# Layer 1's projection back: places freed for its first weights, most of the mixed output split in the attention's last steps, residual read in two parts

## The chip, the cores and the metric

The kernel runs on one core of a Trainium2 chip. The metric is the device time of one execution in microseconds (us); lower is better. Five engines work beside each other, each through its own queue of instructions in order, and meet only at semaphores: PE (matrix products), ACT (activations), DVE (elementwise), POOL (elementwise, slower) and SP, which here only issues DMAs.

## The reference

Two blocks run one after the other on x of 1024 tokens by 1024 features, all in float32. The first block has two layers; the second of them, layer 1, is the one that is touched:

```python
def odd_mixer(h, w_in, sink, w_out, slopes):
    proj = h @ w_in
    qc, kc, vc, gc = jnp.split(proj, [C_Q, C_Q + C_KV, C_Q + 2 * C_KV], axis=-1)
    oc = windowed_sink_attention(qc, kc, vc, sink, slopes)   # 16 heads, 4 key heads, window of 3 blocks of 128
    return (oc * jax.nn.silu(gc)) @ w_out                     # 1024 x 1024
...
x = x + gate * y            # the residual, for which x is needed again
return rms_norm(x, final_norm)
```

The score of a head is q k / 8 plus a bias, minus slope times distance; a sink enters the maximum and the sum. The second block (a recurrence, a gated linear attention, a feed-forward part) follows and is not touched.

## The kernel before, in words

**Split products.** Every product is made of three: a float32 operand is split into a rounded "high" part (fp32r) and the remainder, the "low" part, and PE adds high x high, low x high and high x low. A projection works through output tiles of 128 features. For each, SP loads weights of 128 x 1024 into WR (`sp_weights`), ACT rounds them into WH (`act_high`), POOL makes the remainder WL (`pool_low`), and PE runs 8 steps k with 6 matmuls each of 128x512 (`pe_tile`). WR, WH and WL have two slots each; tile t uses slot t % 2, and its sums lie in two of PSUM's eight banks. `sp_weights(t)` waits until WL of tile t-2 is made.

**The attention of layer 1** (`*_attention_c`) has NG = 32 groups g (4 key heads by 8 blocks of 128 queries) of two units u each (NU = 64). Each engine walks one loop over u, in which the steps of several units are interleaved: in step u PE does the scores of u, turns the probabilities of u-1, spreads the inverse sums of (u-3)/2 and multiplies with the values of group (u-4)/2; DVE adds the bias (`dve_c_bias`), makes the low part of the probabilities (`dve_c_low`), multiplies the gate with the inverse sum (`dve_c_gate`, into C_G) and adds the two halves of the output (`dve_c_add`, into C_O2); ACT does the exponentials (`act_c_raise`, into C_PR), the high part (`act_c_high`) and moves half of the output (`act_c_move`, into C_OT); POOL widens the inverse sums and writes the product of C_O2 and C_G to MIX (`pool_c_mix`, signal c_mixed). After step 63 the loops run on for a few steps until group 31 is done. POOL also makes the bias tables BF and the low parts of keys, queries and values.

MIX, 128 partitions by 8 x 1024, is the mixed output. Its eighths f = 2i and 2i+1 belong to key head i: they are complete when group 8i+7 is.

**The projection back** (`*_odd_out`, tiles ODD_OUT[0] to [7], called tile 0 to 7 here). Tile 0's weights lie in slot 0. It starts when all of MIX is made: `act_odd_out` and `dve_odd_out` first wait for c_mixed(31). ACT then rounds tile 0's weights and the eighths of MIX into HH; DVE clears two buffers, then makes the remainders HL (signal m_low); PE starts step k of tile 0 when m_low(k) is there. SP loads tile 0's weights during the attention, waits for c_mixed(31), issues the reload of the residual X from DRAM ("spill", 4 MB in one DMA), and then the weights of tiles 1 to 7. X lies where the queries of the attention were, so it can't come earlier. DVE adds the residual to each finished tile (`dve_residual`, L398), ACT squares the result, DVE sums the squares for the norm.

**The order of work** is written out by hand: there is no planner. What one engine's instruction needs of another is a wait on a semaphore. Places in SBUF are given in KB per partition by `place(name, kb, shape)`: slot 0 of WH is 127.5 to 131.5, slot 0 of WL 135.5 to 139.5; before the change they are overlaid by BF1 (127.5) and C_PR (133.5).

Of the kernel before, what the change touches and what calls it, by code (L numbers as in the profile page):

```python
# [7 lines left out]
F32 = mybir.dt.float32  # L8
F32R = mybir.dt.float32r
# [122 lines left out]
def build(nc, d, where, known):  # L132
# [111 lines left out]
    def pe_tile(t, high, low, made=None, beside=None):  # L244
        s, w = t % 2, tiles[t]
        pe.wait_ge(*w_low.at(t))
        if t >= 2:
            pe.wait_ge(*evicted(t - 2))
        for k in range(w.kt):
            if made:  # L250
                pe.wait_ge(*made(k))
            for n, (wt, x) in enumerate(((WH, high), (WH, low), (WL, high))):
                for h in range(2):
                    last = pe.matmul(ps[0:w.m, 2 * s + h, :], wt[:, s, k, 0:w.m], x[:, k, halves(h)],  # L254
                                     start=(k == 0 and n == 0), stop=(k == w.kt - 1 and n == 2))
            if k == w.kt - 1:
                last.then_inc(*w_used.up(t))
            if beside:
                beside(k)
# [1134 lines left out]

    NG = C_KV * TT
    NU = 2 * NG
    C_KH, C_KL = place("C_KH", 59, [P, C_KV, SEQ], F32R), place("C_KL", 143.5, [P, C_KV, SEQ], F32R)
    C_QH, C_QL = place("C_QH", 159.5, [P, 4, SEQ], F32R), place("C_QL", 3, [P, DT, SEQ], F32R)
    C_VS = place("C_VS", 175.5, [P, 2, TT, P], F32R)
    C_PTH, C_PTL = place("C_PTH", 183.5, [P, 2, 3, 4, P], F32R), place("C_PTL", 195.5, [P, 2, 3, 4, P], F32R)  # L1400
    C_SB, C_PR = place("C_SB", 51, [P, 4, WIN + 1]), place("C_PR", 133.5, [P, 4, WIN + 1])
    C_OT, C_O2 = place("C_OT", 139.53125, [P, HALF]), [place("C_O20", 141.53125, [P, 2 * P]), place("C_O21", 117.75, [P, 2 * P])]
    AWAY, C_RID, C_G = place("AWAY", 75, [P, WIN]), place("C_RID", 76.5, [P, 2 * P]), place("C_G", 77.5, [P, 2, 2 * P])
    BF = [place("BF0", 111.5, [P, 4, WIN]), place("BF1", 127.5, [P, 4, WIN])]
    C_RS, C_RI, C_NM = (place(n, 117.5 + 0.03125 * i, [P, 2, 4]) for i, n in enumerate(("C_RS", "C_RI", "C_NM")))
    c_tables = signal("c_tables")
    c_scored, c_turned, c_spread, c_summed = signal("c_scored"), signal("c_turned"), signal("c_spread"), signal("c_summed")
# [47 lines left out]
    def pe_c_turn(u):  # L1455
        p = u % 2
        lo, hi, _ = window(u // 2 % TT)
        nk = hi - lo
        pe.wait_ge(*c_raised.at(u, 1))
        if u >= 2:  # L1460
            pe.wait_ge(*c_low.at(u - 2))
        for j in range(2):
            for k in range(nk):
                last = pe.transpose(ps[:, 2 + 2 * p + j, rows(k)], C_PR[:, 2 * p + j, rows(3 - nk + k)], IDENT[:, :])
        last.then_inc(*c_turned.up(u))

    def pe_c_spread(g):
# [33 lines left out]
    def dve_c_bias(u, j):  # L1501

        g, hd = u // 2, 2 * (u % 2) + j
        i, n = g // TT, g % TT
        lo, hi, b0 = window(n)
        w = (hi - lo) * P
        dve.wait_ge(*c_scored.at(u, j))
        if u >= 2:
            dve.wait_ge(*c_raised.at(u - 2, j))
        if n == 0:  # L1510
            dve.wait_ge(*c_bias.at(i, hd))
        dve.tensor_tensor_reduce(C_SB[:, hd, WIN - w:WIN], ps[:, j, 0:w], BF[i % 2][:, hd, b0:b0 + w], -1.0,
                                 NSINK[:, 4 * i + hd:4 * i + hd + 1], ALU.add, ALU.min,
                                 C_NM[:, g % 2, hd:hd + 1]).then_inc(*c_biased.up(u, j))

# [37 lines left out]
    def dve_attention_c():  # L1553
        dve.wait_ge(*c_tables.at(2))
        dve.tensor_scalar(NSINK[:, :], SINK[:, :], -1.0, None, ALU.mult).then_inc(*c_sinks.up())
        for r in range(2):
            dve.wait_ge(*c_key_high.at(0, r))
            dve.tensor_tensor(C_KL[rows(r, HD), 0, :], KC[0:HD, 0, :], C_KH[0:HD, 0, :].bitcast(F32),
                              ALU.subtract).then_inc(*c_key_low0.up(0, r))
        for t in range(2):  # L1560
            dve.wait_ge(*c_query_high.at(t))
            dve.tensor_tensor(C_QL[:, t, :], QC[:, t, :], C_QH[:, t, :].bitcast(F32), ALU.subtract).then_inc(
                *c_query_low0.up(t))
        dve.wait_ge(*c_sinks.at())
        for u in range(NU + 6):
            if u % 2 == 0 and 2 <= u <= NU:
                dve_c_inverse((u - 2) // 2)
            if u < NU:
                dve_c_bias(u, 0)
                dve_c_bias(u, 1)  # L1570
            if 2 <= u < NU + 2:
                dve_c_low(u - 2)
            if u % 2 == 0 and 4 <= u < NU + 4:
                dve_c_gate((u - 4) // 2)
            if u % 2 == 1 and 5 <= u < NU + 5:
                dve_c_add((u - 5) // 2)

    def act_c_keys(i):
        base = (i % 2) * HD
# [14 lines left out]
    def act_c_raise(u, j):  # L1594
        g, hd = u // 2, 2 * (u % 2) + j
        lo, hi, _ = window(g % TT)
        c0 = WIN - (hi - lo) * P
        act.wait_ge(*c_biased.at(u, j))
        if u >= 2:
            act.wait_ge(*c_turned.at(u - 2))  # L1600
        act.activation(C_PR[:, hd, c0:WIN + 1], C_SB[:, hd, c0:WIN + 1], ACT.Exp, bias=C_NM[:, g % 2, hd:hd + 1], scale=-1.0,  # L1601
                       accum_out=C_RS[:, g % 2, hd:hd + 1]).then_inc(*c_raised.up(u, j))

    def act_c_high(u):
# [6 lines left out]
    def act_c_move(g):  # L1611
        act.wait_ge(*c_summed.at(g))
        act.activation(C_OT[0:HD, :], ps[HD:P, 6, :], ACT.Copy).then_inc(*c_moved.up(g))

    def act_attention_c():
        act.wait_ge(*vc_copied.at(1))
        act_c_keys(0)
        for t in range(2):
            act_c_query(t)
        for u in range(NU + 5):  # L1620
            if u % 16 == 0 and u < NU:
                act_c_sinks(u // 16)
                act.wait_ge(*c_sink.at(u // 16))
            if u < NU:
                act_c_raise(u, 0)
                act_c_raise(u, 1)
            if 1 <= u <= NU:
                act_c_high(u - 1)
            if u % 2 == 0 and 4 <= u < NU + 4:
                act_c_move((u - 4) // 2)  # L1630
            i = u // 16 + 1
            if i < C_KV:
                if u % 16 == 5:
                    act_c_keys(i)
                elif u % 16 in (7, 9):
                    act_c_query(2 * i + (u % 16 - 7) // 2)
# [11 lines left out]
    def pool_c_bias(i, hd):  # L1648
        if i >= 2:
            pool.wait_ge(*c_biased.at(16 * (i - 1) - 1, 1))  # L1650
        c_pool_in_turn()
        pool.tensor_scalar(BF[i % 2][:, hd, :], AWAY[:, :], SLOPE[:, 4 * i + hd:4 * i + hd + 1], None, ALU.mult).then_inc(
            *c_bias.up(i, hd))

    def pool_c_keys(i):
# [29 lines left out]
    def pool_attention_c():  # L1685
# [6 lines left out]
        for u in range(NU + 6):  # L1692
# [5 lines left out]
            if i < C_KV:  # L1698
                if u % 16 in (1, 2, 3, 4):
                    pool_c_bias(i, u % 16 - 1)  # L1700
                elif u % 16 == 6:
                    pool_c_keys(i)
                elif u % 16 in (8, 10):
                    pool_c_query(2 * i + (u % 16 - 8) // 2)
                elif u % 16 == 12:
                    pool_c_values(i)

    SQG = place("SQG", 47, [P, 3, SEQ])  # L1710
    SCALE = SQX[:, 1, :]
    sg_made, sg_summed = signal("sg_made"), signal("sg_summed")
    rc_squared, scale_copied, gains_made = signal("rc_squared"), signal("scale_copied"), signal("gains_made")

    def sp_odd_out():
        sp_weights(ODD_OUT[0])
        sp.wait_ge(*c_mixed.at(NG - 1))
        sp.dma_start(X[:, :, :], d["spill"]).then_inc(*x_back.landed(1))
        for t in ODD_OUT[1:]:
            sp_weights(t)  # L1720

    def pe_odd_out():
        pe.wait_ge(*c_added.at(NG - 1))
        for f, t in enumerate(ODD_OUT):
            pe_tile(t, HH, HL, made=(lambda k: m_low.at(1, k)) if f == 0 else None)
        pe_token_sums(2, 4)
        pe_token_sums("gained", 5, SQG, sg_summed)
        pe_spread(2)
# [1 line left out]
        pe_spread("gained")  # L1730

    def act_odd_out():
        act.wait_ge(*c_mixed.at(NG - 1))
        act_high(ODD_OUT[0])
        act_split_mix(1)

        def gained(f):
            act_square("gained", f, SQG, col["final_norm"][:, f:f + 1], sg_made, sg_summed)
# [4 lines left out]

    def pool_odd_out():
        c_pool_in_turn()
        for t in ODD_OUT:
            pool_low(t)

    def dve_odd_out():
        dve.wait_ge(*c_mixed.at(NG - 1))  # L1750
        dve_no_squares(2)
        dve_no_squares("gained", SQG, sg_summed)
        dve_split_mix(1)
        dve.wait_ge(*x_back.at(1))
        for f, t in enumerate(ODD_OUT):
            dve_residual(t, f, MOD[:, 40:48])
            dve_add_square(2, f)
            dve_add_square("gained", f, SQG, sg_made, sg_summed)
# [727 lines left out]
```

## Time and profile before

| | us |
|---|---|
| median of 3 runs | 2632.12 |
| lowest, highest | 2631.97, 2637.21 |
| the profiled execution | 2634.4 |
| its span | 2632.8 |
| PE busy in the span | 2430.4 (92%) |
| DVE, ACT, POOL busy | 1181.5, 1030.4, 666.8 |

The span is the time from the first to the last instruction of the profiled execution; some 1.6 us of that execution lie outside it. All rows below are of this one execution, in us from the span's start. PE is busy for 92% of the span, so what counts is where it waits, and which work of other engines ended the wait.

### The profile page before, as it was taken

How to read it: one execution, taken by the hardware profiler on the slowest of the kernel's cores; microseconds unless marked ns; L12 is line 12 of the kernel's file. 1: busy time of each engine (PE TensorE's matmuls, PEld its weight loads, DVE VectorE, ACT ScalarE, POOL GpSimd, SP SyncE). 2: the span in 40 equal slices, each digit the busy share in tenths (PEclk: the TensorE clock that was granted, in tenths of full speed). 3: DMA queues.
4: the chain of work that ended last, by engine and by line, in shares of the span. 5: the costliest groups of instructions: out<-in, count | busy, mean ns of one | idle time of the engine just before them, and what ended most of it. 6: DMA issues, size and time to landing. Idle time of an engine off the chain costs nothing.

```text
span 2632.8 us, 29952 instructions
## 1 busy us (share of the span) xinstructions
PE 2430.4 (92%) x12026; PEld 1988.4 (76%) x12026; DVE 1181.5 (45%) x1689; ACT 1030.4 (39%) x1533; POOL 666.8 (25%) x449
## 2 busy tenths in 40 slices
PE   3989979979998989988989899999899999999998
PEld 3877668858886768866667677788688888888887
DVE  4714389937885440029963644432422222222224
ACT  3311278848884131139952374131311111111114
POOL 0211124316662112236421211112222222222220
PEclk7999989989999989999999899989899999999999
DMA  7620000000004131100021311003111111111111
GB/s 284 231 74 26 12 1 1 1 17 1 1 1 168 40 104 48 48 20 1 1 97 32 112 45 48 25 25 120 50 44 49 48 49 48 49 48 48 49 45 64
DMA packets 156014, 143.14 MB, mean 54 GB/s; under 512 B 9798, under 2 KB 140132, under 8 KB 153956
## 3 DMA queue, kind: packets, MB, share of 16 engines
q1 hardware_dynamic: 155876, 141.22, 16.4%
q8 instruction: 96, 1.57, 0.2%
q14 instruction: 42, 0.34, 0.0%
HBM read 124.43 MB, written 16.78 MB: 54 GB/s over the span
## 4 chain that ended last, share of the span: by engine, by line
PE 80%; ACT 7%; DVE 7%; issue 4%; DMA 1%; POOL 1%; SPq 0%; ACTq 0%; DVEq 0%; POOLq 0%
PE ps L254 52%; PE ps L2259 9%; PE ps L1013 4%; PE ps L1036 3%; PE ps L1023 3%; ACT C_PR L1601 1%; DVE T L369 1%; PE ps L1882 1%; ACT C_PTH L1609 1%; PE ps L1870 1%; PE ps L336 1%; PE ps L1485 1%; ACT B_PR L1100 1%; PE ps L729 1%; DMA WR<-in_odd_w_out 1%
## 5 line engine op out<-in xcount | busy, mean ns | idle before, releaser
L241 POOL TENSOR_TENSOR WL<-WR,WH 128x1024 fp32r<-128x1024 f32 (+2 forms) x137 | 320.3, 2338 | 1199.1 <-ACT WH L236 1199.1
L254 PE MATMUL ps<-HH,WH 128*128 128x512 f32 (+1 forms) x1200 | 386.5, 404 | 48.8 <-DVE HL L394 17.6
L254 PE MATMUL ps<-HL,WH 128*128 128x512 f32 (+1 forms) x1200 | 377.1, 396 | 0.0
L254 PE MATMUL ps<-HH,WL 128*128 128x512 f32 (+1 forms) x1200 | 374.9, 394 | 0.0
L254 PEld LDWEIGHTS ps<-HH,WH 128*128 128x128 f32 (+1 forms) x1200 | 222.8, 190 | 108.2 <-issue 38.7
L254 PEld LDWEIGHTS ps<-HL,WH 128*128 128x128 f32 (+1 forms) x1200 | 228.6, 191 | 50.9
L254 PEld LDWEIGHTS ps<-HH,WL 128*128 128x128 f32 (+1 forms) x1200 | 228.0, 190 | 50.8
L254 PE MATMUL ps<-HHF,WH 128*128 128x512 f32 x704 | 218.4, 391 | 7.4 <-DVE HLF L374 6.9
L254 PE MATMUL ps<-HLF,WH 128*128 128x512 f32 x704 | 217.7, 390 | 0.0
L254 PE MATMUL ps<-HHF,WL 128*128 128x512 f32 x704 | 217.3, 390 | 0.0
L2302 DVE TENSOR_TENSOR AT<-SG,ps 128x1024 f32<-128x1024 f32 x22 | 26.9, 1221 | 418.9 <-PE ps L254 418.9
L2274 ACT ACTIVATE SG<-ps 128x1024 f32<-128x1024 f32 x22 | 22.6, 1029 | 384.1 <-PE ps L254 384.1
L1051 DVE TENSOR_REDUCE NM<-ps 128x1 f32<-128x1024 f32 x128 | 156.2, 1220 | 33.3 <-PE ps L1013 32.7
L254 PEld LDWEIGHTS ps<-HHF,WH 128*128 128x128 f32 x704 | 132.1, 188 | 37.0 <-DVE HLF L374 5.0
L2307 DVE TENSOR_TENSOR XF<-ps,XF 128x1024 f32<-128x1024 f32 x88 | 107.7, 1224 | 105.8 <-PE ps L2259 105.0
L254 PEld LDWEIGHTS ps<-HLF,WH 128*128 128x128 f32 x704 | 132.7, 189 | 27.8
L254 PEld LDWEIGHTS ps<-HHF,WL 128*128 128x128 f32 x704 | 132.7, 188 | 27.8
L236 ACT ACTIVATE WH<-WR 128x1024 fp32r<-128x1024 f32 (+2 forms) x137 | 136.0, 994 | 39.0 <-issue 10.3
L2292 POOL TENSOR_TENSOR OWL<-OW,OWH 128x2048 fp32r<-128x2048 f32 x11 | 50.7, 4608 | 305.4 <-ACT OWH L2279 305.4
L2259 PE MATMUL ps<-AH,OWH 128*128 128x512 f32 x352 | 110.4, 395 | 0.0
L2259 PE MATMUL ps<-AL,OWH 128*128 128x512 f32 x352 | 109.8, 393 | 0.2
L2259 PE MATMUL ps<-AH,OWL 128*128 128x512 f32 x352 | 108.7, 390 | 0.0
(370 smaller groups left out, 4379.6 us busy)
## 6 DMA issues: line engine op xcount, KB each, us to landing
WR<-in_w_ffn_in SPq DMA_DIRECT2D x44, 512.0 KB, 3.7
AW<-in_ada_w SPq DMA_DIRECT2D x8, 2048.0 KB, 9.0
spill<-X SPq DMA_DIRECT2D x3, 4096.0 KB, 13.3
OW<-in_w_ffn_out SPq DMA_DIRECT2D x11, 1024.0 KB, 6.0
WR<-in_w_in SPq DMA_DIRECT2D x21, 512.0 KB, 3.7
WR<-in_odd_w_in SPq DMA_DIRECT2D x20, 512.0 KB, 3.7
WR<-in_even_w_in SPq DMA_DIRECT2D x17, 512.0 KB, 3.7
AWK<-in_ada_w SPq DMA_DIRECT2D x8, 1024.0 KB, 9.4
```

What stands on the lines that cost most here:

```text
L236: act.activation(WH[:, s, 0:w.kt, 0:w.m], WR[:, s, 0:w.kt, 0:w.m], ACT.Copy).then_inc(*w_high.up(t))
L241: pool.tensor_tensor(WL[:, s, 0:w.kt, 0:w.m], WR[:, s, 0:w.kt, 0:w.m], WH[:, s, 0:w.kt, 0:w.m].bitcast(F32), ALU.subtract).then_inc(*w_low ...
L254: last = pe.matmul(ps[0:w.m, 2 * s + h, :], wt[:, s, k, 0:w.m], x[:, k, halves(h)], start=(k == 0 and n == 0), stop=(k == w.kt - 1 and n = ...
L336: last = pe.matmul(ps[:, bank, t:t + 1], buffer[:, 2, rows(t)], ONEC[:, 0:1], start=True, stop=True)
L1013: last = pe.matmul(ps[:, b + j, :], qs[:, rows(q)], ks[:, halves(j)], start=(n == 0), stop=(n == len(passes) - 1))
L1023: last = pe.transpose(ps[:, 4 + j, rows(k)], D.PR[:, p % 3, rows(4 * j + k)], IDENT[:, :])
L1036: last = pe.matmul(ps[:, 6 + pg % 2, 0:2 * P], D.VS[:, D.v_of(h), k, :], pt[pg % 2][:, k, :], start=(k == 0 and n == 0), stop=(k == TT - 1 ...
L1051: dve.tensor_reduce(NM[:, s % 4:s % 4 + 1], pair(2 * (s % 2)), AX_X, ALU.max, negate=True).then_inc(*m_done.up(g, s))
L2259: last = pe.matmul(ps[:, 4 + 2 * (n % 2) + h, :], w[:, k, rows(n)], x[:, k, halves(h)], start=(k == 0 and m == 0), stop=(k == 1 and m == 2))
L2292: pool.tensor_tensor(OWL[:, :, :], OW[:, :, :], OWH[:, :, :].bitcast(F32), ALU.subtract).then_inc(*ow_low.up(i))
L2302: dve.tensor_tensor(AT[:, v, :], SG[:, v, :], pair(2 * (t % 2)), ALU.mult).then_inc(*ev_dve.up(t))
L2307: dve.tensor_tensor(LAST.x[:, n, :], pair(4 + 2 * (n % 2)), LAST.x[:, n, :], ALU.add).then_inc(*y_added.up(i, n))
```

## The change

Four things are done.

The bias tables and the exponentials get other places, so that the slots 0 of WH and WL are free from unit 32 on: the tables of key head 3 go to BF3 at 3 KB, the exponentials of the units from 32 on to C_PR1 at 9 KB. The high parts of MIX get places of their own, HO (16 KB over the low and 16 KB over the high keys), and the low parts, LO, replace MIX in place. Keys are read by the scores up to unit 63, so HO can be written from step 64 on.

Tile 0's weights are rounded by ACT in step 64 and their remainder is made by POOL in step 66. Eighths 0 and 1 of MIX are split by ACT in step 65, eighths 2 and 3 in step 67; DVE makes the low parts of eighths 0 and 1 in steps 65 and 66. The remaining eighths follow in `act_odd_out` and `dve_odd_out`, each waiting for its own part of MIX.

The residual is read by two DMAs, of two eighths and of six, with a signal each. `pe_odd_out` waits for the last bias operation (which read banks 0 and 1) instead of the last add.

```diff
@@ pe_tile @@
+            xh, xl = (x[k] if isinstance(x, list) else x[:, k, :] for x in (high, low))
+            for n, (wt, x) in enumerate(((WH, xh), (WH, xl), (WL, xh))):
@@ places @@
-    C_SB, C_PR = place("C_SB", 51, [P, 4, WIN + 1]), place("C_PR", 133.5, [P, 4, WIN + 1])
+    C_SB = place("C_SB", 51, [P, 4, WIN + 1])
+    C_PRS = [place("C_PR0", 133.5, [P, 4, WIN + 1]), place("C_PR1", 9, [P, 4, WIN + 1])]
+    BF += [BF[0], place("BF3", 3, [P, 4, WIN])]
+    HO0, HO1 = place("HO0", 143.5, [P, 4, SEQ], F32R), place("HO1", 59, [P, 4, SEQ], F32R)
+    HO, LO = [(HO0, HO1)[f % 2][:, f // 2, :] for f in range(DT)], place("LO", 79.5, [P, DT, SEQ], F32R)
@@ dve_attention_c, at the end of step u @@
+            if u in (NU + 1, NU + 2):
+                dve_c_split(u - NU - 1)
@@ new @@
+    def act_c_split(f):
+        act.wait_ge(*c_mixed.at(8 * (f // 2) + 7))
+        act.activation(HO[f], MIX[:, f, :], ACT.Copy).then_inc(*m_high.up(1, f))
+
+    def dve_c_split(f):
+        dve.wait_ge(*m_high.at(1, f))
+        dve.tensor_tensor(LO[:, f, :], MIX[:, f, :], HO[f].bitcast(F32), ALU.subtract).then_inc(*m_low.up(1, f))
@@ act_attention_c, behind the move of step u @@
+            if u == NU:
+                act_high(ODD_OUT[0])
+            elif u in (NU + 1, NU + 3):
+                act_c_split(u - NU - 1)
+                act_c_split(u - NU)
@@ pool_attention_c, at the end of step u @@
+            if u == NU + 2:
+                c_pool_in_turn()
+                pool_low(ODD_OUT[0])
+                pool.wait_ge(*w_low.at(ODD_OUT[0]))
@@ sp_odd_out @@
-        sp.dma_start(X[:, :, :], d["spill"]).then_inc(*x_back.landed(1))
+        sp.dma_start(X[:, 0:2, :], d["spill"][:, 0:2, :]).then_inc(*x_two.landed())
+        sp.dma_start(X[:, 2:DT, :], d["spill"][:, 2:DT, :]).then_inc(*x_back.landed(1))
@@ pe_odd_out @@
-        pe.wait_ge(*c_added.at(NG - 1))
+        pe.wait_ge(*c_biased.at(NU - 1, 1))
-            pe_tile(t, HH, HL, made=(lambda k: m_low.at(1, k)) if f == 0 else None)
+            pe_tile(t, HO, LO, made=(lambda k: m_low.at(1, k)) if f == 0 else None)
@@ act_odd_out @@
-        act.wait_ge(*c_mixed.at(NG - 1))
-        act_high(ODD_OUT[0])
-        act_split_mix(1)
+        for f in range(4, DT):
+            act_c_split(f)
@@ pool_odd_out @@
-        for t in ODD_OUT:
+        for t in ODD_OUT[1:]:
@@ dve_odd_out @@
-        dve.wait_ge(*c_mixed.at(NG - 1))
+        for f in range(2, DT):
+            dve_c_split(f)
         dve_no_squares(2)
         dve_no_squares("gained", SQG, sg_summed)
-        dve_split_mix(1)
-        dve.wait_ge(*x_back.at(1))
         for f, t in enumerate(ODD_OUT):
+            if f == 0:
+                dve.wait_ge(*x_two.at())
+            elif f == 2:
+                dve.wait_ge(*x_back.at(1))
```

The new actions in the order of each queue: DVE in step 65 the low part of unit 63, the add of group 30, split 0; in step 66 the gate of group 31, split 1; in step 67 the add of group 31. POOL in step 65 the product of group 30, in step 66 the remainder of tile 0's weights, in step 67 the product of group 31.

## Rows read from the trace of the kernel before

**Rows 1.** The page's section 4: the chain of waits by line.
```profile
PE ps L254 52%; PE ps L2259 9%; PE ps L1013 4%; PE ps L1036 3%; PE ps L1023 3%; ACT C_PR L1601 1%; DVE T L369 1%; PE ps L1882 1%; ACT C_PTH L1609 1%; PE ps L1870 1%; PE ps L336 1%; PE ps L1485 1%; ACT B_PR L1100 1%; PE ps L729 1%; DMA WR<-in_odd_w_out 1%
```
**Rows 2.** The chain in order of time, 1343 to 1440: start, us, what.
```profile
1343.57 0.74 POOL MIX L1682
...
1344.33 0.33 SPq L1718
...
1344.70 14.95 DMA WR<-in_odd_w_out
...
1359.67 1.07 ACT WH L236
...
1363.23 76.47 PE ps L254 x336
```
**Rows 3.** Timeline of PE at tile 1's start: start, us, engine, line, [idle <-releaser].
```profile
1363.23 0.73 PE L254 MATMUL ps<-HH,WH 128*128 128x512 f32 x2 [0.89 <-POOL WL L241]
```
**Rows 4.** Timeline of the attention's tail on ACT, DVE and POOL.
```profile
1339.20 0.59 ACT L1613 ACTIVATE C_OT<-ps 64x512 f32<-64x512 f32 x1 [1.15 <-PE ps L1485]
...
1340.71 0.42 DVE L1539 TENSOR_TENSOR C_G<-ps,MIX 128x256 f32<-128x256 f32 x1
1340.76 0.74 POOL L1682 TENSOR_TENSOR MIX<-C_O,C_G 128x256 f32<-128x256 f32 x1 [1.98 <-DVE C_O L1550]
...
1342.02 0.59 ACT L1613 ACTIVATE C_OT<-ps 64x512 f32<-64x512 f32 x1 [2.23 <-PE ps L1485]
1342.65 0.85 DVE L1550 TENSOR_TENSOR C_O<-ps,C_OT 64x256 f32<-64x256 f32 x2 [1.51 <-ACT C_OT L1613]
```
**Rows 5.** Timeline behind the last product: ACT's splits and POOL's remainder.
```profile
1345.29 7.67 ACT L389 ACTIVATE HH<-MIX 128x1024 fp32r<-128x1024 f32 x8
1345.53 2.36 POOL L241 TENSOR_TENSOR WL<-WR,WH 128x1024 fp32r<-128x1024 f32 x1 [1.23 <-ACT WH L236]
```
**Rows 6.** Timeline of DVE: its first split, and its first two merged.
```profile
1346.48 2.49 DVE L394 TENSOR_TENSOR HL<-MIX,HH 128x1024 fp32r<-128x1024 f32 x1
...
1346.48 3.62 DVE L394 TENSOR_TENSOR HL<-MIX,HH 128x1024 fp32r<-128x1024 f32 x2
```
**Rows 7.** Timeline of the same pair in layer 0.
```profile
822.86 2.35 POOL L241 TENSOR_TENSOR WL<-WR,WH 128x1024 fp32r<-128x1024 f32 x1 [5.19 <-ACT WH L236]
...
823.69 2.60 DVE L394 TENSOR_TENSOR HL<-MIX,HH 128x1024 fp32r<-128x1024 f32 x1 [4.84 <-ACT HH L389]
```
**Rows 8.** Timeline of PE: two neighbouring pairs of tile 0.
```profile
1351.81 1.06 PE L254 MATMUL ps<-HH,WH 128*128 128x512 f32 x2
...
1352.67 1.05 PE L254 MATMUL ps<-HL,WH 128*128 128x512 f32 x2
```
**Rows 9.** Windows: PE, PEld, DVE, ACT, POOL busy; granted clock; DMA share, GB/s.
```profile
1343.00:1344.00 1.00, 0.00 (x0) 0.00 (x0) 0.48 (x2) 0.00 (x0) 0.43 (x1) 0.67 0.00 0
...
1349.00:1350.00 1.00, 0.88 (x2) 0.82 (x3) 1.00 (x1) 1.00 (x2) 0.00 (x0) 0.50 1.06 459
...
1353.00:1354.00 1.00, 1.00 (x4) 0.75 (x4) 1.00 (x2) 0.00 (x0) 0.00 (x0) 0.71 1.20 508
```
**Rows 10.** X's landing; XF's first issue, its second part's landing (L2177), weights behind.
```profile
DMA to landing us min/median/max: 13.6/13.6/13.6
...
1776.59 0.34 SPq L2176 DMA_DIRECT2D XF<-spill  x1
...
DMA to landing us min/median/max: 11.8/11.8/11.8
...
1791.84 1.06 ACT L236 ACTIVATE WH<-WR 128x1024 fp32r<-128x1024 f32 x1 [1.97 <-DMA WR<-in_w_out]
```
**Rows 11.** Windows in which PE started after a pause and in which the clock rose.
```profile
1462.00:1463.00 1.00, 0.43 (x1) 0.46 (x2) 0.96 (x2) 0.36 (x1) 0.00 (x0) 0.50 0.48 112
1466.00:1467.00 1.00, 1.00 (x5) 0.64 (x4) 1.00 (x2) 0.77 (x1) 0.00 (x0) 0.89 0.05 12
```

More of the change, by code:

```diff
@@ L251, in pe_tile @@
                 pe.wait_ge(*made(k))
-            for n, (wt, x) in enumerate(((WH, high), (WH, low), (WL, high))):
+            xh, xl = (x[k] if isinstance(x, list) else x[:, k, :] for x in (high, low))
+            for n, (wt, x) in enumerate(((WH, xh), (WH, xl), (WL, xh))):
                 for h in range(2):
-                    last = pe.matmul(ps[0:w.m, 2 * s + h, :], wt[:, s, k, 0:w.m], x[:, k, halves(h)],
+                    last = pe.matmul(ps[0:w.m, 2 * s + h, :], wt[:, s, k, 0:w.m], x[:, halves(h)],
                                      start=(k == 0 and n == 0), stop=(k == w.kt - 1 and n == 2))
@@ L1396, in build @@
     NU = 2 * NG
+    NU_HALF = NU // 2
     C_KH, C_KL = place("C_KH", 59, [P, C_KV, SEQ], F32R), place("C_KL", 143.5, [P, C_KV, SEQ], F32R)
@@ L1463, in pe_c_turn @@
             for k in range(nk):
-                last = pe.transpose(ps[:, 2 + 2 * p + j, rows(k)], C_PR[:, 2 * p + j, rows(3 - nk + k)], IDENT[:, :])
+                last = pe.transpose(ps[:, 2 + 2 * p + j, rows(k)], C_PRS[u // NU_HALF][:, 2 * p + j, rows(3 - nk + k)], IDENT[:, :])
         last.then_inc(*c_turned.up(u))
@@ L1511, in dve_c_bias @@
             dve.wait_ge(*c_bias.at(i, hd))
-        dve.tensor_tensor_reduce(C_SB[:, hd, WIN - w:WIN], ps[:, j, 0:w], BF[i % 2][:, hd, b0:b0 + w], -1.0,
+        dve.tensor_tensor_reduce(C_SB[:, hd, WIN - w:WIN], ps[:, j, 0:w], BF[i][:, hd, b0:b0 + w], -1.0,
                                  NSINK[:, 4 * i + hd:4 * i + hd + 1], ALU.add, ALU.min,
@@ L1600, in act_c_raise @@
             act.wait_ge(*c_turned.at(u - 2))
-        act.activation(C_PR[:, hd, c0:WIN + 1], C_SB[:, hd, c0:WIN + 1], ACT.Exp, bias=C_NM[:, g % 2, hd:hd + 1], scale=-1.0,
+        act.activation(C_PRS[u // NU_HALF][:, hd, c0:WIN + 1], C_SB[:, hd, c0:WIN + 1], ACT.Exp, bias=C_NM[:, g % 2, hd:hd + 1], scale=-1.0,
                        accum_out=C_RS[:, g % 2, hd:hd + 1]).then_inc(*c_raised.up(u, j))
@@ L1651, in pool_c_bias @@
         c_pool_in_turn()
-        pool.tensor_scalar(BF[i % 2][:, hd, :], AWAY[:, :], SLOPE[:, 4 * i + hd:4 * i + hd + 1], None, ALU.mult).then_inc(
+        pool.tensor_scalar(BF[i][:, hd, :], AWAY[:, :], SLOPE[:, 4 * i + hd:4 * i + hd + 1], None, ALU.mult).then_inc(
             *c_bias.up(i, hd))
@@ L1712, in build @@
     sg_made, sg_summed = signal("sg_made"), signal("sg_summed")
+    x_two = signal("x_two")
     rc_squared, scale_copied, gains_made = signal("rc_squared"), signal("scale_copied"), signal("gains_made")
```

## The prediction, made before the changed kernel ran

> **What bounds the kernel now.** I read the page's chain of waits first, to see which work sets the end. PE's projections (L254) hold 52% of it, and of the stage that is changed the chain lists a transfer, the load of projection weights, at about 1% [rows 1]. The same chain in order of time shows how that transfer gets there: the last group of layer 1's attention ends with the product on POOL at 1343.57, SP then issues the reload of the residual at 1344.33, and the weights of output tile 1, queued behind it at 1344.70, land 14.95 us later. ACT rounds them (1.07), POOL makes the remainder (2.36 for tile 0's, [rows 5]), and from 1363.23 PE runs 336 matmuls, the seven tiles 1 to 7, without a break for 76.47 us [rows 2]. So the stage has one gate, the start of tile 1. Everything that tile 0 does before is beside it: between tile 0 and tile 1 PE did wait for 0.89 us, and what ended the wait was POOL's WL [rows 3].
>
> I write G for the end of the last attention product (1344.31 before; c_mixed(31) in the code). Tile 1 starts at G plus 18.9 us: 15.34 from SP's first issue to ACT's start on the weights of tile 1, then 3.6 for ACT and POOL (1359.67 to 1363.23). The question for each part of the change is therefore: does it move G, or the 18.9, or the speed of PE behind it?
>
> **The change part by part.**
>
> *New places for the bias and the exponentials (BF, C_PR).* The same instructions write to and read from other addresses; no wait is added, no instruction either. I cost it at nothing.
>
> *Tile 0's weights made early.* ACT's rounding of them (1.07 us in the chain, [rows 2]) now stands behind the move of group 30, which ended at 1339.79. ACT has 2.23 us free there before the next move [rows 4], so it ends at about 1340.8 and harms nobody by itself. POOL's remainder of 2.36 us now stands between the product of group 30 (ends 1341.50) and that of group 31 (1343.57): 1341.66 to 1344.03. Alone it would push the product of group 31, and so G, by 0.46 us. It is hidden behind what follows on DVE.
>
> *Splits 0 and 1 in the loop's last steps.* On ACT each takes 0.96 us (7.67 for eight, [rows 5]). Behind the rounding they run to about 1341.75 and 1342.7, and the last move, which began at 1342.02, comes at about 1342.65: 0.6 late, if nothing else were. On DVE the order counts. Split 0 stands in front of the gate of group 31, split 1 between that gate and the add of group 31, and behind the add stands the product that is G. The gate could run at 1340.71 before [rows 4]; now it stands behind split 0, which waits for ACT until 1341.8.
>
> And split 0 will not start then. At that moment POOL is in its remainder of tile 0's weights. In the trace DVE's first split took 2.49 us, where the next one added 1.13: POOL's remainder ran 1345.53 to 1347.89 and the split ended 1.08 after it [rows 5, 6]. In layer 0 the same pair repeats: POOL until 825.21, the split of 2.60 us ends at 826.29, again 1.08 after [rows 7]. So a subtraction of two SBUF operands on DVE does not overlap POOL's subtraction; it is held until POOL has ended. Placed here: POOL ends 1344.03, split 0 ends 1345.11, gate (0.42) 1345.55, split 1 (1.13, and some 0.1 in which neighbours overlap) 1346.75, and the add of group 31 starts there instead of at 1342.65. G is 4.1 us late, at 1348.4. Bounds for this term: 0.6 if DVE's order cost nothing and ACT's move alone were late; 5.3 if split 1 is held by a further 1.2 us. I take 4.1.
>
> The start of POOL (1341.66) and of split 0 (1341.8) lie only 0.14 us apart, so the other order must be priced. Both rows have POOL first; none here shows what POOL does when DVE is first. If the two then ran side by side at full speed, split 0 would be ended at 1343.0, and that is the first rival below. By the Trainium skill (SBUF — State Buffer, the part on the port pair that DVE and GpSimd share) whoever starts first has the pair for the whole instruction and the other blocks. By that rule split 0 would end 1343.0, POOL 1345.4, split 1 (blocked meanwhile) 1346.45, and G would be 3.8 late instead of 4.1: the order hardly matters.
>
> *Tile 0 on PE.* It waits for WL (1344.03) and split 0 (1345.11). Its k-steps are then paced by DVE: splits 2 to 7 follow the late add, 1.14 us apart [rows 6], the last at about 1354.8. PE needs 6 matmuls a step, 0.86 us for two at the low clock (1351.81 to 1352.67, [rows 8]) and 0.455 at the high (76.47 us for 336, [rows 2]). The clock fell to half at 1343.3 in the trace [rows 9]; it will be low again for the first two steps. Tile 0 ends at about 1358, against 1362.3 before (0.89 us ahead of 1363.23). That gain of 4 us buys nothing, because tile 1's weights are not there.
>
> *Residual read in two.* SP issues one more DMA (0.33 us, [rows 2]) ahead of tile 1's weights. The last stage has the same pattern already: XF in 1024 KB and 3072 KB, then weights. From its first issue at 1776.59 to ACT's start on the weights behind it are 15.25 us [rows 10], against 15.34 here; so nothing either way, from 1.4 less (X landed 13.6 us after its issue, XF's second part 11.8 after an issue that stood some 0.4 behind the first: 12.2, [rows 10]) to 0.4 more. That the residual's first two eighths are there earlier helps only tile 0's evacuation, which before waited for PE, and which nobody needs before tile 2.
>
> *PE's clock at tile 1.* This is the cover that goes. Before, PE went from tile 0 to tile 1 with a gap of 0.89 us, and the tiles behind it ran at 0.455 us for two matmuls, the high clock (2.4 GHz) [rows 2, 3]; the low clock fell entirely into tile 0, where it cost nothing. Now PE stands from about 1358 to 1367.3, some 9 us. After the pause before tile 0, from 1342.0, when ACT's last move was released [rows 4], to 1349.12, the clock was 0.50 (1.2 GHz), and came back in 1353 to 1354, 4.5 us after the first matmul (0.71 in that window is the change at 1353.58) [rows 9]. Another start after a pause was at 0.50 for 3.7 us (1462.57 to 1466.22 by the windows' shares) [rows 11]. At the low clock 1 - 0.455/0.86 = 47% of the time is lost: 2.1 and 1.7 us. I take 2.0, nearer to the start in this stage. Tile 1 carries that on the path. Bounds: 0 if the clock holds, 2.5 if it stays low as much longer than 4.5 us as the other start was shorter.
>
> *Behind it.* Tiles 2 to 7, their weights, the token sums and the rest of the program run as before, later.
>
> **The sum.** 4.1 (G) + 0 (transfers) + 2.0 (clock) = +6.1 us. Made against the profiled execution of 2634.4 us (span 2632.8) it gives 2640.5. That execution is 2.3 us above the median of the runs, 2632.1, so in the medians' terms the forecast is 2632.1 + 6.1 = 2638.2 us.
>
> **The rivals.**
>
> 1. *G is late by half.* DVE and POOL overlap here, or ACT's splits come sooner: then split 0 ends 1343.0, the gate 1343.45, split 1 1344.6, the add starts 1344.7: G +2.0. With the clock's 2.0 it is +4.0, 2636.1. Against it are the two rows of 2.49 and 2.60 us [rows 6, 7].
>
> 2. *The clock holds.* G +4.1 alone, 2636.2. For it: PE's last matmul before the low clock lay 1.3 us back and the change came inside a pause of 7 us, so a shorter pause may pass. Against it: the pause here is longer than that one.
>
> 3. *The other side: not slower.* The reload in two parts lands sooner, as the XF pair did (12.2 us against 13.6), and takes tile 1's weights with it by 1.4 us. This wins from the point where G is less than 1.4 us late and the clock is paid back; it needs DVE to take its two splits in time that it had idle (1.51 us before the last add, [rows 4]). At G unchanged it gives -1.4, 2630.7. Against it: the weights behind XF came at 15.25, hardly sooner than here, and the two splits hold 2.3 us of work in front of the add, more than the idle time.
>
> 4. *More than the sum.* The second DMA issue costs its 0.4 us on top, split 1 is held as well (1.2), the clock takes 2.5: +8.2, 2640.3.
>
> **How the numbers follow.** Forecast with its own spread of 5 to 7 us: 0.55. Rival 1: 0.17, rival 2: 0.08, rival 3: 0.08, rival 4: 0.12. The measurement can tell about 0.2%, 5.3 us, from no change, and the forecast lies just beyond it. Of the forecast's 0.55 some 0.41 lie above 5.3, with rival 4's 0.12 that is 0.53 for slower. Rivals 1 and 2, the forecast's lower end and most of rival 3 give 0.44 for no difference. Faster by over 5.3 us has no mechanism that I can price: 0.03. The range runs from 2633.5 (G late by 1.4 us and nothing lost to the clock) to 2641.5 (rival 4 and the spread of the runs); it leaves out rival 3 and little else. So the direction is slower, by an amount at the edge of what can be told.
>
> **What would show it.** In the trace of the changed kernel: the last MIX product on POOL ends 4 us later counted from the move of group 30; DVE's first split next to POOL's remainder lasts about 3.3 us, though its two operands are there; the DMA of tile 1's weights still takes about 15 us and ACT's WH and POOL's WL follow it; PE pauses about 9 us between tile 0 and tile 1; and the granted clock is 0.50 for the first 4 us of tile 1. The forecast is wrong if tile 1 starts less than 3 us later than before, seen from the move of group 30, or if the clock behind the pause is 1.00, or if tile 1 waits for something else than its WL.

## The result and the profile after

Over 22 runs of each kernel in turn, the changed one took 2637.26 us in the median (2632.12 to 2644.44), the kernel before 2632.06 (2628.87 to 2637.49). The ratio is 1.0019 with a 95% interval of 1.0011 to 1.0026: the change makes the kernel 5.0 us slower (2.9 to 6.8).

The profiled execution of the changed kernel took 2634.11 us with a span of 2632.5 us, no longer than the one of before (2634.4, 2632.8). So it can't be read by its span; the stage has to be read by itself. Both traces have a common mark ahead of every action that was added or moved: ACT's move of group 30. It starts at 1339.20 before [rows 4] and at 1339.92 here. I call it M and give all times of the stage from it. Only the new places for the bias and the exponentials lie ahead of it, and they cost nothing: from ACT's move of group 8, well ahead of unit 32, to M it is 114.93 us in both traces.

The chain of waits in order of time, changed kernel, 1341 to 1447 (start, us, what). It is the counterpart of [rows 2]:

```profile
1343.42 4.68 issue x2
1348.10 1.72 POOL MIX L1704
...
1349.84 0.33 SPq L1745
...
1350.20 0.43 SPq L1746
...
1350.68 13.12 DMA WR<-in_odd_w_out
...
1363.82 1.06 ACT WH L236
...
1365.02 2.36 POOL WL L241
...
1367.43 78.79 PE ps L255 x336
```

The reload is issued at M + 9.92 instead of M + 5.13. ACT starts on tile 1's weights 13.98 us later (15.34 before). Tile 1 starts at M + 27.51 instead of M + 24.03, and the seven tiles behind it take 78.79 us instead of 76.47. Together 3.48 + 2.32 = 5.8 us by the end of tile 7.

The timeline of the attention's tail in the changed kernel, the counterpart of [rows 4] to [rows 6]:

```profile
1339.92 0.59 ACT L1621 ACTIVATE C_OT<-ps 64x512 f32<-64x512 f32 x1 [1.16 <-PE ps L1491]
1340.41 1.04 ACT L236 ACTIVATE WH<-WR 128x1024 fp32r<-128x1024 f32 x1
...
1341.36 1.99 ACT L1626 ACTIVATE HO<-MIX 128x1024 fp32r<-128x1024 f32 x2
1341.47 0.74 POOL L1704 TENSOR_TENSOR MIX<-C_O,C_G 128x256 f32<-128x256 f32 x1 [2.00 <-DVE C_O L1556]
...
1342.29 2.36 POOL L241 TENSOR_TENSOR WL<-WR,WH 128x1024 fp32r<-128x1024 f32 x1
...
1342.44 3.30 DVE L1630 TENSOR_TENSOR LO<-MIX,HO 128x1024 fp32r<-128x1024 f32 x1 [1.05 <-ACT HO L1626]
1343.25 0.58 ACT L1621 ACTIVATE C_OT<-ps 64x512 f32<-64x512 f32 x1
...
1345.66 0.41 DVE L1545 TENSOR_TENSOR C_G<-ps,MIX 128x256 f32<-128x256 f32 x1
...
1345.99 1.21 DVE L1630 TENSOR_TENSOR LO<-MIX,HO 128x1024 fp32r<-128x1024 f32 x1
...
1347.12 0.84 DVE L1556 TENSOR_TENSOR C_O<-ps,C_OT 64x256 f32<-64x256 f32 x2
...
1347.99 7.44 DVE L1630 TENSOR_TENSOR LO<-MIX,HO 128x1024 fp32r<-128x1024 f32 x6
1348.10 1.71 POOL L1704 TENSOR_TENSOR MIX<-C_O,C_G 128x256 f32<-128x256 f32 x1 [3.44 <-issue]
```

POOL's remainder runs from 1342.29 to 1344.65. DVE's split 0 starts 0.15 us after it and ends at 1345.74, 1.09 after POOL: 3.30 us for an operation that takes 1.21 two rows further down. Gate, split 1 and add follow, and the add of group 31 starts at M + 7.20, where it started at M + 3.45. The last row shows what I had not counted: POOL's last product takes 1.71 instead of 0.74, because DVE had begun split 2 0.11 us before it.

Windows of the changed kernel (busy of PE, PEld, DVE, ACT, POOL; granted clock; DMA share, GB/s) are the counterpart of [rows 9]:

```profile
1367.00:1368.00 1.00, 0.57 (x1) 0.50 (x2) 1.00 (x1) 0.81 (x1) 0.48 (x2) 0.50 0.00 0
1371.00:1372.00 1.00, 1.00 (x4) 0.80 (x3) 0.77 (x1) 0.00 (x0) 0.00 (x0) 0.50 0.16 47
1372.00:1373.00 1.00, 1.00 (x5) 0.79 (x4) 0.00 (x0) 0.00 (x0) 0.00 (x0) 0.83 0.82 246
```

After a pause of 7.59 us tile 1 begins at the low clock. The granted 0.83 of the last window puts the change to the high one at 1372.34, so the low clock lasted 4.9 us.

Where did these 5.8 us go, if the spans are equal? M itself came 0.7 us later. The first 0.8 us came back at once, in the sums behind tile 7. There too the clock fell. In the kernel before it fell while PE still stood (granted 0.66 in 1442 to 1443, PE began at 1443.40), in the changed one about 1 us after PE had begun (0.93 in 1450 to 1451, begun at 1449.92). The first row is the kernel before, the second, in a fence of its own, the changed one:

```profile
1443.40 3.57 PE L336 MATMUL ps<-ONEC,SQX 128*128 128x1 f32 x16 [3.72 <-DVE SQX L331]
```

```profile
1449.92 2.76 PE L337 MATMUL ps<-ONEC,SQX 128*128 128x1 f32 x16 [3.73 <-DVE SQX L332]
```

From there to 1700 the changed kernel is 5.0 us behind, counted from M. Then 2.7 us come back in the second block, because 32 matmuls of 64 columns (line 1882, 1912 in the changed kernel) happened to run at another clock. Again the kernel before stands first:

```profile
1721.00:1725.00 4.00, 4.00 (x19) 4.00 (x20) 0.00 (x0) 0.00 (x0) 0.00 (x0) 0.50 0.48 131
```

```profile
1727.00:1731.00 4.00, 4.00 (x34) 3.85 (x33) 0.00 (x0) 0.00 (x0) 0.00 (x0) 0.93 0.42 121
```

The same 32 matmuls took 7.09 us in one trace and 3.97 in the other. Nothing near them was changed. Smaller differences of this kind follow, and by the end the changed kernel's trace is 1.0 us ahead, counted from M. The runs of one kernel spread over 9 to 12 us, and one chance of this kind is enough for a quarter to a third of that; one execution can't carry a verdict of 5.

### The profile page after: what moved, and what is told of

It reads as the page before. It is cut to its first block, busy times and chain, and to the rows that moved or that the text cites. A ratio compares the mean times of both kernels' runs of the same rounds, so it can differ in the third digit from the quotient of the medians.

```text
span 2632.5 us, 29955 instructions
## 1 busy us (share of the span) xinstructions
PE 2424.7 (92%) x12026; PEld 1982.2 (75%) x12026; DVE 1186.0 (45%) x1689; ACT 1030.0 (39%) x1533; POOL 667.1 (25%) x449
## 4 chain that ended last, share of the span: by engine, by line
PE 80%; ACT 7%; DVE 6%; issue 4%; DMA 1%; POOL 1%; SPq 0%; ACTq 0%; DVEq 0%; POOLq 0%
PE ps L255 52%; PE ps L2289 9%; PE ps L1014 4%; PE ps L1037 3%; PE ps L1024 3%; ACT C_PR L1609 1%; DVE T L370 1%; ACT B_PR L1101 1%; ACT B_PTH L1095 1%; ACT C_PTH L1617 1%; PE ps L1491 1%; PE ps L1900 1%; PE ps L1912 1%; PE ps L730 1%; PE ps L1470 1%
## 5 line engine op out<-in xcount | busy, mean ns | idle before, releaser
L255 PE MATMUL ps<-HH,WH 128*128 128x512 f32 (+1 forms) x1072 | 346.2, 405 | 41.9 <-DVE HL L375 14.8
L255 PE MATMUL ps<-HL,WH 128*128 128x512 f32 (+1 forms) x1072 | 336.3, 395 | 0.0
L255 PE MATMUL ps<-HH,WL 128*128 128x512 f32 (+1 forms) x1072 | 334.7, 394 | 0.0
L255 PEld LDWEIGHTS ps<-HH,WH 128*128 128x128 f32 (+1 forms) x1072 | 198.8, 191 | 95.6 <-issue 31.5
L255 PEld LDWEIGHTS ps<-HL,WH 128*128 128x128 f32 (+1 forms) x1072 | 203.8, 190 | 45.7
L255 PEld LDWEIGHTS ps<-HH,WL 128*128 128x128 f32 (+1 forms) x1072 | 203.1, 189 | 45.4
```

## The experiments

Eight kernels were run, each against the kernel before on the same chip. The table gives, from their traces and from M: the issue of the reload, the time from there to ACT's start on tile 1's weights, the start of tile 1, the time of tiles 1 to 7, the end of tile 7 and its difference from before; and the measured ratio. Where the weights of tile 1 come ahead of the reload, there is no such transfer to time, and the next two columns give the start of tile 0 and the time of all eight tiles.

| kernel | reload | to WH | start | tiles | end | against before | ratio, 95% interval |
|---|---|---|---|---|---|---|---|
| before | 5.13 | 15.34 | 24.03 | 76.47 | 100.50 | | |
| changed | 9.92 | 13.98 | 27.51 | 78.79 | 106.30 | +5.8 | 1.0019 [1.0011, 1.0026] |
| e1 splits behind | 6.42 | 14.55 | 24.57 | 78.09 | 102.66 | +2.2 | 1.0005 [0.9996, 1.0014] |
| e4 remainder behind | 7.84 | 15.33 | 26.81 | 76.48 | 103.29 | +2.8 | 1.0010 [1.0001, 1.0019] |
| e3 one reload | 9.91 | 14.16 | 27.67 | 78.75 | 106.42 | +5.9 | 1.0011 [1.0002, 1.0021] |
| e6 kept busy | 9.92 | 13.90 | 27.46 | 76.47 | 103.93 | +3.4 | 1.0008 [1.0000, 1.0017] |
| e8 order only | 6.17 | 13.92 | 23.70 | 77.90 | 101.60 | +1.1 | 1.0002 [0.9993, 1.0012] |
| e5 before, weights first | 5.12 | | tile 0: 9.91 | all: 89.09 | 99.00 | -1.5 | 0.9994 [0.9986, 1.0003] |
| e2 weights first | 9.91 | | tile 0: 5.96 | all: 90.12 | 96.08 | -4.4 | 0.9986 [0.9977, 0.9995] |
| e7 order and weights | 6.17 | | tile 0: 3.53 | all: 89.94 | 93.47 | -7.0 | 0.9976 [0.9966, 0.9986] |

(0.001 of the time is 2.6 us.)

M has to be as good a mark in the other kernels. From ACT's move of group 22 to M it is 40.04 us before and 39.96 to 40.10 in all others but e7 and e8, where it is 40.60. Those two make tile 0's remainder on POOL in step 47, and the 0.5 us are lost right there, between the moves of groups 22 and 24. So against a mark ahead of that step e8 stands at +1.7 and e7 at -6.5, instead of the table's +1.1 and -7.0.

**The splits behind the last add (e1).**

```diff
 # dve_attention_c
-            if u in (NU + 1, NU + 2):
-                dve_c_split(u - NU - 1)
 # act_attention_c
-            elif u in (NU + 1, NU + 3):
-                act_c_split(u - NU - 1)
-                act_c_split(u - NU)
+            elif u == NU + 3:
+                for f in range(4):
+                    act_c_split(f)
 # dve_odd_out
-        for f in range(2, DT):
+        for f in range(DT):
```

> The changed kernel with one thing moved: ACT's splits 0 and 1 stand behind the move of group 31, DVE's splits 0 and 1 behind the add of group 31. Tile 0's weights are still made in steps 64 and 66, the reload is still in two. Theory (the place of the splits on DVE, next to POOL's remainder, is what makes the last product late): SP's reload is issued 5.1 to 6.2 us after the start of the move of group 30, as in the kernel before (5.13), not 9.92 as in the changed one; tile 1 starts about 23.5 us after that move instead of 27.5; some clock cost stays (about 2 us), so the time is 4 us under the changed kernel, about +1 us against the kernel before (ratio 1.0004). Rival (POOL's remainder between the two products is what delays, wherever the splits stand): the reload stays at 8 us or later and the time at +4 to +5 us.

The reload is issued at M + 6.42, 3.5 us sooner than in the changed kernel, and the time is +1.3 us (-1.1 to +3.7) against before. The rival, that POOL's remainder alone makes the delay, falls. But 6.42 lies outside the 5.1 to 6.2 that were expected: the reload is still 1.3 us late. Of these 0.4 are POOL's remainder in front of the last product (the forecast had 0.46 for that), and most of the rest is the hold in the other direction. The timeline of e1:

```profile
1343.41 2.36 POOL L241 TENSOR_TENSOR WL<-WR,WH 128x1024 fp32r<-128x1024 f32 x1
...
1345.43 9.90 DVE L1628 TENSOR_TENSOR LO<-MIX,HO 128x1024 fp32r<-128x1024 f32 x8
1345.85 1.59 POOL L1702 TENSOR_TENSOR MIX<-C_O,C_G 128x256 f32<-128x256 f32 x1
```

DVE began its splits at 1345.43. POOL's last product came 0.42 later, right behind the remainder, and took 1.59 us instead of 0.74.

**The remainder behind the last product (e4).**

```diff
 # pool_attention_c
-            if u == NU + 2:
+            if u == NU + 3:
                 c_pool_in_turn()
                 pool_low(ODD_OUT[0])
```

> The changed kernel with POOL's remainder of tile 0's weights made behind the product of group 31 instead of in front of it. It tells the two halves of the late product apart: the hold of DVE's split 0 by POOL, and the mere order of the splits on DVE. Theory (both count): split 0 takes 1.2 us instead of 3.3, so the reload is issued about 7.8 us after the start of the move of group 30 (9.92 in the changed kernel, 5.13 before), tile 1 starts about 25.5 us after it (27.5, 24.0); tile 0 starts later, so the pause before tile 1 shrinks to some 4 us and may or may not cost clock: time +1.5 to +3.7 us against the kernel before, ratio 1.0010. Rival (the hold alone counts): the reload at 5.9 us or less. Rival (the order alone counts): no change, 9.9 us, ratio 1.0019.

The first split of e4 lasts 1.22 us, and the reload is issued at M + 7.84:

```profile
1342.30 1.22 DVE L1630 TENSOR_TENSOR LO<-MIX,HO 128x1024 fp32r<-128x1024 f32 x1 [1.05 <-ACT HO L1626]
...
1347.62 0.33 SPq L1745 DMA_DIRECT2D X<-spill  x1
...
1347.67 3.21 POOL L241 TENSOR_TENSOR WL<-WR,WH 128x1024 fp32r<-128x1024 f32 x1
...
1366.59 0.72 PE L255 MATMUL ps<-HO,WH 128*128 128x512 f32 x2 [1.65 <-POOL WL L241]
```

So 9.92 - 7.84 = 2.1 us of the delay of 4.8 are the hold of split 0 by POOL's remainder; the other 2.7 are the two splits' place in front of the gate and the add, and the held product. Tile 0 started late in this kernel, the pause before tile 1 was 1.65 us (about 4 were expected), and the seven tiles took 76.48 us: no clock was lost. Tile 1 started at M + 26.81 and not at 25.5, because the transfer took 15.33 us; see e3.

**PE kept busy in the pause (e6).** The 32 added matmuls write to banks that nothing reads before tile 1 overwrites them.

```diff
 # pe_odd_out
             pe_tile(t, HO, LO, made=(lambda k: m_low.at(1, k)) if f == 0 else None)
+            if f == 0:
+                for r in range(32):
+                    pe.matmul(ps[:, 2 + r % 2, :], HO[0][:, 0:P], HO[1][:, halves(r // 2 % 2)], start=True, stop=True)
```

> The changed kernel with 32 more matmuls of 128x512 on PE between tile 0 and tile 1, 7.3 us at the high clock, into tile 1's two banks, from where nothing reads them. They fill the pause of 7.59 us and change nothing else. Theory (the pause lets the clock fall, and tile 1 pays about 2.3 us for it): the granted clock stays 1.00 into tile 1, the seven tiles 1 to 7 take 76.5 us again instead of 78.8, and the time is 2.3 us under the changed kernel, about +2.7 us against the kernel before (ratio 1.0010). Rival (the clock's level at tile 1 does not hang on the pause, or what it costs here it gives back later): no difference from the changed kernel, +5 us.

The timeline and a window of e6:

```profile
1360.71 7.42 PE L1756 MATMUL ps<-HO,HO 128*128 128x512 f32 x32
1369.10 0.73 PE L255 MATMUL ps<-HO,WH 128*128 128x512 f32 x2 [0.97 <-POOL WL L241]
```

```profile
1369.00:1370.00 1.00, 0.90 (x4) 0.77 (x5) 1.00 (x1) 0.45 (x1) 0.52 (x2) 1.00 0.00 0
```

Tile 1 starts where it did (M + 27.46) and the clock is 1.00; the seven tiles take 76.47 us, exactly as before, instead of 78.79. The ratio falls from 1.0019 to 1.0008, by 2.9 us. The two intervals overlap, so the time alone would not decide, but the trace does.

**One reload (e3).**

```diff
 # sp_odd_out
-        sp.dma_start(X[:, 0:2, :], d["spill"][:, 0:2, :]).then_inc(*x_two.landed())
-        sp.dma_start(X[:, 2:DT, :], d["spill"][:, 2:DT, :]).then_inc(*x_back.landed(1))
+        sp.dma_start(X[:, :, :], d["spill"]).then_inc(*x_back.landed(1))
...
 # dve_odd_out
             if f == 0:
-                dve.wait_ge(*x_two.at())
-            elif f == 2:
                 dve.wait_ge(*x_back.at(1))
```

> The changed kernel with the residual read by one DMA again. In the changed kernel ACT started on tile 1's weights 13.98 us after the reload's issue, against 15.34 before. Theory A (reading in two made it sooner): here it is 15.3 again, tile 1 starts 1.4 us later than in the changed kernel and the time is +6.4 us against the kernel before (ratio 1.0024). Theory B (transfers of this kind vary by that much from one execution to the next, whatever their number): 13.5 to 15.5 here, and the time is that of the changed kernel, +5 us (ratio 1.0019).

ACT starts on tile 1's weights 14.16 us after the issue, well inside the range of the five kernels that read in two (13.90 to 15.33). The ratio is 1.0011 and its interval ends at 1.0021, below the 1.0024 of theory A. Theory A falls: reading in two brought nothing and cost nothing that can be told.

Whether the 1.4 us between 15.34 and 13.98 are mere spread is another question, and theory B is not shown. Counted from the reload's first issue, the last part of X landed after 13.6 us in three traces (before, e5 and e4) and after 12.1 to 12.8 in the other seven. Those three are the kernels in which POOL makes tile 0's remainder, and PE begins tile 0, only after the issue. On the other hand a transfer which nothing here touches, layer 0's reload of X, also landed anywhere from 14.0 to 15.5 us after its issue in the ten traces. With one trace of each kernel the two can't be told apart.

**Tile 1's weights first (e2), and the same edit on the kernel before (e5).**

```diff
 # sp_odd_out
         sp_weights(ODD_OUT[0])
+        sp_weights(ODD_OUT[1])
         sp.wait_ge(*c_mixed.at(NG - 1))
...
-        for t in ODD_OUT[1:]:
+        for t in ODD_OUT[2:]:
```

> The changed kernel, with the weights of tile 1 loaded ahead of the wait for the last product, so ahead of the reload. Theory (tile 1 was held only by its weights queued behind the reload, and the clock fell in the pause that this made): tile 1 follows tile 0 within 1 us, the clock stays at 1.00 through tiles 1 and 2, tile 2 starts at about 1371 us if tile 0 starts at 1346, its own weights now coming 19 us after the late reload; the time is 9 us under the changed kernel, -4 us against the kernel before (ratio 0.9985). Rival (the late product also holds tile 2, or something else on ACT or POOL holds tile 1): tile 1 or tile 2 still waits 3 us or more for WL, and the time is no better than the kernel before.

> The kernel before with one thing changed: tile 1's weights are loaded ahead of the wait for the last product. Theory (before, tile 0 and the transfer were nearly level, so the transfer alone was worth only the 0.89 us that PE waited): tile 1 follows tile 0 at once, seen from the move of group 30 at 23.1 us instead of 24.0, the time is 0.9 us less, ratio 0.9997. Rival (the early load brings more, as the gain of the changed kernel with the same edit, 8 us, might suggest): ratio 0.9985 or less.

In e2 the chain runs through tile 0 without a pause to the end of tile 7:

```profile
1345.98 3.30 DVE LO L1630
...
1349.42 90.12 PE ps L255 x384
```

The time is -3.7 us (-6.1 to -1.3) against before; the late reload, at M + 9.91 as in the changed kernel, holds nobody now. On the kernel before the same edit gives -1.6 us (-3.7 to +0.8), which can't be told from nothing. Its trace shows 1.5: the 0.9 us pause is gone, tile 0 is at the low clock for 3.7 us instead of 4.5, which is 0.3 us, and the remaining 0.3 can't be given to one thing. So the early start of tile 0 was real in the changed kernel, and this transfer was what made it worthless.

**Another order (e8), and both (e7).** ACT's split 0 now stands behind its high part of unit 63, ahead of the move of group 30.

```diff
 # act_attention_c
+            if u == NU:
+                act_c_split(0)
...
-            if u == NU:
+            if u == 45:
                 act_high(ODD_OUT[0])
-            elif u in (NU + 1, NU + 3):
-                act_c_split(u - NU - 1)
-                act_c_split(u - NU)
+            elif u == NU + 1:
+                act_c_split(1)
+                act_c_split(2)
+            elif u == NU + 3:
+                act_c_split(3)
 # dve_attention_c (dve_odd_out then takes 1 to 7)
-            if u in (NU + 1, NU + 2):
-                dve_c_split(u - NU - 1)
+            if u == NU + 2:
+                dve_c_split(0)
 # pool_attention_c
-            if u == NU + 2:
+            if u == 47:
                 c_pool_in_turn()
                 pool_low(ODD_OUT[0])
 # e7 alone, sp_odd_out
         sp_weights(ODD_OUT[0])
+        sp_weights(ODD_OUT[1])
+        sp_weights(ODD_OUT[2])
         sp.wait_ge(*c_mixed.at(NG - 1))
...
-        for t in ODD_OUT[1:]:
+        for t in ODD_OUT[3:]:
```

> The changed kernel with another order in the attention's last steps: tile 0's weights are rounded in step 45 and their remainder made in step 47; ACT makes split 0 between its high part of unit 63 and the move of group 30, splits 1 and 2 behind it; DVE makes split 0 between the gate and the add of group 31, where it stood idle for 1.5 us, and split 1 behind the add. SP's order is that of the changed kernel. Theory (the last product sets tile 1 through the transfer; tile 0 is beside it): the reload is issued about 6.2 us after the start of the move of group 30, tile 0 starts at about 3.2 us after it, tile 1 at 24 to 25; a pause of some 8 us before tile 1 costs 2 us: time about +2 us against the kernel before, ratio 1.0008. Rival (tile 0 starting 6 us before it did brings some of them): ratio under 0.9990.

> The order of the previous kernel, and the weights of tiles 1 and 2 loaded ahead of the wait for the last product. Theory (with the transfer out of the way PE's own work from the attention's last values on is the bound, and each us that tile 0 starts sooner counts in full): tile 0 starts about 3.2 us after the start of the move of group 30 (9.9 before), the clock stays up or falls only for tile 0, the last tile ends about 92 us after it (100.5 before): time 8 us under the kernel before, ratio 0.9970. Rival (something else comes up: the rounding in step 45 delays the attention, POOL's remainder for tile 1 is held by DVE's splits, or DVE's splits pace tile 0): at most the 4 us of the kernel with tile 1's weights first, ratio 0.9985.

e8 starts tile 0 at M + 3.53, 6.4 us sooner than the kernel before did, and is no faster: 1.0002, or +0.5 us (-1.8 to +3.2). Its rival, under 0.9990, falls. The pause before tile 1 is 7.96 us and costs 1.4 (77.90 against 76.47), not the 2 that were expected. e7 takes the transfer away as well and has the lowest ratio of all: 2628.5 us against 2634.9, -6.3 us (-9.0 to -3.7). Timeline of e7:

```profile
1343.93 1.53 DVE L1630 TENSOR_TENSOR LO<-MIX,HO 128x1024 fp32r<-128x1024 f32 x1
...
1345.62 0.70 PE L255 MATMUL ps<-HO,WH 128*128 128x512 f32 x2 [0.74 <-DVE LO L1630]
...
1346.41 10.78 DVE L1630 TENSOR_TENSOR LO<-MIX,HO 128x1024 fp32r<-128x1024 f32 x7
...
1351.36 2.47 POOL L241 TENSOR_TENSOR WL<-WR,WH 128x1024 fp32r<-128x1024 f32 x1 [3.13 <-ACT WH L236]
...
1354.97 0.74 PE L255 MATMUL ps<-HO,WH 128*128 128x512 f32 x2 [1.22 <-DVE LO L1630]
```

The clock was 1.00 in every window between 1343 and 1360, so tile 0 ran at the high clock from its start. I had hoped for 8 us. One was lost where POOL's remainder of tile 1 held a split for 3.41 us instead of 1.21, so that PE waited 1.22 us in tile 0; the 0.5 us in step 47 were lost on top. The measured interval reaches from the 8 us of the theory to the 4 of its rival and overlaps e2's, so that e7 beats e2 is shown by the traces (-6.5 against -4.4) and not by the times.

## Why the prediction was right, point by point

- *The gate is the start of tile 1, through the transfer behind the reload.* Right. e8 moved tile 0 by 6.4 us and the time by nothing that can be told; e2 moved the transfer and won 8.7 us over the changed kernel (0.9986 against 1.0019, each against the kernel before, so give or take 3 us).
- *New places at nothing.* Right: 114.93 us from the move of group 8 to M in both traces.
- *G is 4.1 us late.* The sum was 0.7 too small: the reload came 4.8 us later. The add of group 31 starts 3.75 later (I had 4.1); what was not in the sum is the last product on POOL, held by DVE's split 2 for another 1.0 us. I had priced the hold for DVE behind POOL and, for the reverse, only at split 0. The forecast of 3.3 us for split 0 met 3.30. The rule of the Trainium skill (SBUF — State Buffer, on the shared port pair), that whoever comes first has it for the whole instruction, fits the reverse rows as well: POOL's product began 0.11 us (changed kernel) and 0.42 us (e1) behind a split of DVE and took 1.71 and 1.59 us instead of 0.74. Both ended 0.6 us after that split, a little less than the length of the product alone, so hardly any of it was done before the split ended.
- *The transfers at 0.* This term was mis-sized: it came out 1.36 less in this trace. The range that I gave (1.4 less to 0.4 more) held it, but not for its reason: it was no effect of reading in two (e3). Whether it was the spread of such transfers, or came from POOL's remainder and tile 0 now standing ahead of the reload, is open.
- *The clock at 2.0.* It was 2.32, over a low stretch of 4.9 us, behind a pause of 7.59 us (I had about 9). e6 shows that the pause causes it and that filling the pause gives it back in full; e4, with a pause of 1.65 us, lost none. Rival 2 falls. The price does not follow the length of the pause alone: 5.09 us cost 1.6 (e1), 7.96 us cost 1.4 (e8), 7.71 us cost 2.3 (e3).
- *Rival 1* (DVE and POOL overlap) falls with the 3.30 us and with e4. *Rival 3* had its price, 1.36 us, by chance or for another reason, and its mechanism wrong. *Rival 4*'s held split was split 2 holding POOL, not split 1 being held.
- *The sum* of +6.1 stands against +5.8 in the trace and +5.0 (2.9 to 6.8) measured. That it came so near is in part luck: two errors, 0.7 and 0.3 too little, met one of 1.4 too much. That the time lay at the edge of what can be told was right too.

What stays open: the last 0.8 us between the trace's +5.8 and the measured +5.0 lie inside the interval. This one trace gives 0.8 back in the sums behind tile 7, as e3's does (5.9 to 5.1), but in e4, e5, e6, e7 and e8 nothing changes there, so whether it belongs to the change is not shown. That a split waits for the port, rather than for something else that POOL's subtraction occupies, is not shown by these runs either: they show that the two exclude each other.

## What to carry to other kernels

Starting a stage earlier is worth nothing while its second tile waits for a transfer queued behind something that the first one does not need; look in the chain for the wait behind the one that you remove, and put small loads that the next tile needs ahead of a large one that waits (here two lines were worth 8.7 us on top of the change; without it 1.6, which can't be told from nothing). Work put "beside" an engine's tail has an order: if it stands in front of the last steps that release a DMA, the DMA pays, and a pause that this opens on PE can be paid a second time through the clock. On DVE and POOL, look at whether two operations with both operands in SBUF meet, in both directions. A mark for comparing traces has to lie ahead of the change in each of them: M did not in e7 and e8, and hid 0.5 us.

## What the runs showed of the hardware

- A DVE subtraction with both operands in SBUF and a POOL operation exclude each other: split 0 took 3.30 us next to POOL's remainder of 2.36 and 1.22 without it; POOL's product took 1.59 to 1.77 us next to DVE's splits and 0.74 without them. A held split ended 1.08 us after POOL's operation, a held product 0.6 us after DVE's split. The gate, with one operand in PSUM, ran beside POOL's product and neither was longer: 0.42 and 0.74 us at 1340.7 [rows 4].
- 4 MB and 0.5 MB behind it, read from DRAM, took 13.90 to 15.34 us until the reader of the last 0.5 MB started, in seven traces, whether the 4 MB were one DMA (14.16, 15.34) or two (13.90 to 15.33). The two above 15 are before and e4, the kernels in which POOL's remainder ran behind the issue; that this is the cause is not shown.
- After a pause of 7.59 us PE ran its first 4.9 us at the low clock; after pauses of 0.97 and 1.65 us it ran at the high one. In e1, after a pause of 5.09 us, it started tile 1 (1365.61) at the high clock and lost it some 0.1 us later: granted 0.86 in 1365 to 1366, 0.50 in the three windows behind, 0.94 in 1369 to 1370, 1.6 us lost over the seven tiles. So the clock can fall after the work has begun again; in the sums behind tile 7 of the changed kernel, begun at 1449.92, it was 1.00 in 1449 to 1450, 0.93 in 1450 to 1451 and 0.50 behind that.
- Equal spans can hide 5 us, most of it through the clock: in the second block 32 small matmuls took 7.09 us at the low clock in one trace and 3.97 at the high one in the other.
